# Half pieces of projection work in the latent scan, and an earlier load of attention's operands

## The reference

```python
proj = h @ p['w_in']
q, k, v, z, xbc, dt, gates = jnp.split(proj, SPLIT_IDX, axis=-1)
...
y_f, h_f = ssd_chunked(xs, dt_f, a[0], bm, cm, h0_f)      # scan over chunks of 128 tokens,
y_b, h_b = ssd_chunked(flip(xs), flip(dt_b), ...)         # forward and backward
y = y_f + flip(y_b) + p['d_skip'].astype(jnp.float32)[:, None] * xs
y = rms_norm(y * jax.nn.silu(z), p['ssd_norm'])
g_a, g_b = jnp.split(gates, 2, axis=-1)
merged = jax.nn.sigmoid(g_a) * (attn @ p['w_attn_o']) + jax.nn.sigmoid(g_b) * (y @ p['w_ssd_o'])
```

## Time and profile before

| | us |
|---|---|
| median of 3 runs | 1606.64 |
| the runs | 1606.43, 1606.64, 1609.6 |
| the profiled execution | 1606.35 |
| its span, first to last instruction | 1604.7 |
| PE, DVE, ACT busy in the span | 1545.9, 970.6, 616.4 |
| chunks 1 to 4 on PE, start to start | 52.4, 54.0, 53.9, 46.8 |

### The profile page before, as it was taken

One profiled execution on the slowest core, in us unless ns is written; L12 is line 12 of the kernel. 1 busy time (PEld: TensorE's weight loads), 2 busy tenths in 40 slices (PEclk: granted clock), 3 DMA queues, 4 the chain that ended last, 5 costly groups with the idle time before them and its releaser, 6 DMA issues.

```text
span 1604.7 us, 27065 instructions
## 1 busy us (share of the span) xinstructions
PE 1545.9 (96%) x11130; PEld 1470.5 (92%) x11130; DVE 970.6 (60%) x1359; ACT 616.4 (38%) x1112; POOL 98.7 (6%) x155
## 2 busy tenths in 40 slices
PE   4999999999999999999999999999999999999997
PEld 3899999999999989999655899999999999999997
DVE  5666666668564798898465452448863343442478
ACT  2433333343562366767466343233421121221120
POOL 1001122100101000000000010000000000000000
PEclk9999999999999999999999999999999999999999
DMA  9555455543858668865701345324122222123221
GB/s 318 176 198 189 147 191 171 187 139 103 286 185 287 240 208 281 248 205 168 275 27 45 128 139 186 128 90 163 54 79 79 80 79 80 54 79 106 79 80 66
DMA packets 159910, 241.62 MB, mean 151 GB/s; under 512 B 8080, under 2 KB 126592, under 8 KB 156736
## 3 DMA queue, kind: packets, MB, share of 16 engines
q1 hardware_dynamic: 136624, 171.45, 32.1%
q0 software_dynamic: 12304, 47.72, 8.2%
q10 hardware_dynamic: 10880, 20.97, 5.0%
HBM read 195.06 MB, written 45.06 MB: 150 GB/s over the span
## 4 chain that ended last, share of the span: by engine, by line
PE 84%; DVE 6%; ACT 5%; DMA 2%; issue 1%; SPq 1%; ACTq 0%; DVEq 0%
PE acc L859 67%; PE tp L859 13%; ACT arena L1740 2%; PE tp L1301 1%; DMA arena<-decay_sums_t 1%; DVE wlo L2011 1%; PE tp L987 1%; DMA arena<-in_w_mod 1%; DVE arena L2116 1%; ACT whi L1518 1%; ACT whi L1877 1%; DVE wlo L2467 1%; PE tp L1348 1%; DVE arena L2285 1%; PE tp L898 0%
## 5 line engine op out<-in xcount | busy, mean ns | idle before, releaser
L859 PE MATMUL acc<-hh,whi 128*128 128x322 f32 x1152 | 301.1, 320 | 6.5 <-issue 4.5
L859 PE MATMUL acc<-hl,whi 128*128 128x322 f32 x1152 | 294.8, 315 | 0.0
L859 PE MATMUL acc<-hh,wlo 128*128 128x322 f32 x1152 | 293.5, 313 | 0.0
L859 PEld LDWEIGHTS acc<-hh,whi 128*128 128x128 f32 x1152 | 203.1, 192 | 11.4 <-issue 9.0
L2011 DVE TENSOR_TENSOR wlo<-raw,whi 128x2048 fp32r<-128x2048 f32 x74 | 169.3, 2288 | 61.4 <-ACT whi L1518 61.4
L859 PEld LDWEIGHTS acc<-hl,whi 128*128 128x128 f32 x1152 | 204.6, 192 | 0.0
L859 PEld LDWEIGHTS acc<-hh,wlo 128*128 128x128 f32 x1152 | 204.4, 192 | 0.0
L1518 ACT ACTIVATE whi<-raw 128x2048 fp32r<-128x2048 f32 x74 | 141.1, 1907 | 162.3 <-PE acc L859 161.9
L859 PE MATMUL acc<-whi,hh 128*128 128x256 f32 x640 | 183.1, 286 | 0.0
L859 PE MATMUL acc<-whi,hl 128*128 128x256 f32 x640 | 179.8, 281 | 0.0
L859 PE MATMUL acc<-wlo,hh 128*128 128x256 f32 x640 | 179.7, 281 | 0.0
(11 more groups left out here) (278 smaller groups left out, 2672.4 us busy)
## 6 DMA issues: line engine op xcount, KB each, us to landing
raw<-in_w_in SPq DMA_DIRECT2D x38, 1024.0 KB, 8.6
raw<-in_w_mlp SPq DMA_DIRECT2D x32, 1024.0 KB, 5.3
arena<-in_w_mod SPq DMA_DIRECT2D x24, 1024.0 KB, 8.2
arena<-decay_sums_t ACTq DMA_DIRECT2D x40, 512.0 KB, 6.3
arena<-xs_nat SPq DMA_DIRECT2D x8, 1024.0 KB, 10.6
raw<-in_w_ssd_o SPq DMA_DIRECT2D x8, 1024.0 KB, 6.2
y_nat<-arena POOLq DMA_DIRECT2D x6, 1024.0 KB, 5.6
arena<-y_nat SPq DMA_DIRECT2D x6, 1024.0 KB, 5.9
```

Source lines behind the costliest of these rows:

```text
L859: return pe.matmul(out, l, r, start=first, stop=last)
```

## The change

The table now counts half pieces. `F_LAT` is 4 and `F_LAT_G` = [2, 0, 2, 1, 2, 2, 2, 2]: as before in halves, but for one half more ahead of group 3. That is 17 halves a chunk, 34 pieces in four chunks instead of 32, and `F_END` is 2 instead of 4. A half is the contraction over k = 0 to 3 or 4 to 7 of a piece, 12 matmuls; the waits stand ahead of the first half and the signal behind the second. ACT, DVE, POOL and SP deal with a piece where its second half is (`ended`). In chunks 2 and 4 a call of two halves is the end of one piece and the beginning of the next.

On SP, the loads that belong to the last 8 pieces (two blocks of `w_attn_o`) stand behind attention's loads (`until`). On DVE, `lower_owed` of the last block stands behind the first two row maxima.

```diff
-        F_LAT = [2, 2, 2, 2]
-        F_LAT_G = [1, 0, 1, 0, 1, 1, 1, 1]
-        F_END = N_ZP + N_GP - (F_CTX + sum(F_CTX_G) + F_H0 + 12 * F_BACK + sum(F_LAT) + 4 * sum(F_LAT_G))
+        F_LAT, F_LAT_G = 4, [2, 0, 2, 1, 2, 2, 2, 2]
+        N_PIECES = N_ZP + N_GP
+        F_END = N_PIECES - (F_CTX + sum(F_CTX_G) + F_H0 + 12 * F_BACK + 2 * (F_LAT + sum(F_LAT_G)))
+        def ended(halves, n):
+            k = halves["k"]
+            halves["k"] += n
+            return halves["k"] // 2 - k // 2
...
+            until = N_ZP + N_GP - 8
+            def weights_to_come(n):
+                weights(min(ended(halves, n), until - pieces["k"]))
             for c in range(1, NT):
-                weights(F_LAT[c - 1])
+                weights_to_come(F_LAT)
...
                 for g in range(NG):
-                    weights(F_LAT_G[g])
+                    weights_to_come(F_LAT_G[g])
...
             sp.dma_start(qT[:, 2:HQ], heads[:, 2:HQ]).then_inc(s["av_in"], 16)
-            weights(F_END)
+            weights(N_PIECES - pieces["k"])
...
-            def gate_piece(n):
+            def gate_piece(n, ks=range(KT)):
...
-                if n % 4 == 0:
-                    pe.wait_ge(lo["sem"], due(lo))
-                step(free)
-                pe.wait_ge(free["sem"], value(free, 2))
-                for k in range(KT):
+                if 0 in ks:
+                    if n % 4 == 0:
+                        pe.wait_ge(lo["sem"], due(lo))
+                    step(free)
+                    pe.wait_ge(free["sem"], value(free, 2))
+                for k in ks:
...
-                last.then_inc(ready["sem"], step(ready))
+                if KT - 1 in ks:
+                    last.then_inc(ready["sem"], step(ready))
...
+            def fill_halves(n):
+                for _ in range(n):
+                    ks = (range(0, KT // 2), range(KT // 2, KT))[halves["k"] % 2]
+                    p = pieces["k"]
+                    if p < N_ZP:
+                        z_tile(p, ks)
+                    else:
+                        gate_piece(p - N_ZP, ks)
+                    step(pieces, ended(halves, 1))
...
             for c in range(1, NT):
-                fill(1)
+                fill_halves(2)
...
-                fill(F_LAT[c - 1] - 1)
+                fill_halves(F_LAT - 2)
                 pe.wait_ge(bnin[b]["sem"], due(bnin[b]))
                 for g in range(NG):
-                    fill(F_LAT_G[g])
+                    fill_halves(F_LAT_G[g])
                     scan_group(g, b, c)
...
             weights(F_END)
-            lower_owed()
...
             maxima(0)
             maxima(1)
+            lower_owed()
```

More of the change, by code:

```diff
@@ L579, in z_in @@
                 sp.dma_start(zq[:, q % 2], z_d[c][:, q * 512:(q + 1) * 512]).then_inc(s[f"zq_in{q % 2}"], 16)
+            halves = {"k": 0}
+            until = N_ZP + N_GP - 8
+            def weights_to_come(n):
+                weights(min(ended(halves, n), until - pieces["k"]))
             for c in range(1, NT):
-                weights(F_LAT[c - 1])
+                weights_to_come(F_LAT)
                 if 1 < c < NT - 1:
@@ L824, in _ @@
             stores(4 * F_BACK)
+            halves = {"k": 0}
             for c in range(1, NT):
-                stores(F_LAT[c - 1] + sum(F_LAT_G))
+                stores(ended(halves, F_LAT + sum(F_LAT_G)))
                 if c < NT - 1:
@@ L1096, in _, with z_tile @@
             pieces = count(s["acc_ready"])
-            def z_tile(p):
+            def z_tile(p, ks=range(KT)):
                 slot, t, u = p // NT % 2, p % NT, p % 2
-                if t == 0:
-                    pe.wait_ge(lo["sem"], due(lo))
-                step(free)
-                pe.wait_ge(free["sem"], value(free, 2))
-                for k in range(KT):
+                if 0 in ks:
+                    if t == 0:
+                        pe.wait_ge(lo["sem"], due(lo))
+                    step(free)
+                    pe.wait_ge(free["sem"], value(free, 2))
+                for k in ks:
                     for m, w in ((hh, whi), (hh, wlo), (hl, whi)):
@@ L1791, in _ @@
                     weights(F_BACK)
+            halves = {"k": 0}
             for c in range(1, NT):
                 exps(NG * c)
-                weights(1)
+                weights(ended(halves, 2))
                 if c > 1:
@@ L1797, in _ @@
                 exps(NG * c + 1)
-                weights(1)
+                weights(ended(halves, F_LAT - 2))
                 if c > 1:
                     squares(c - 1, 3, zq[:, 1])
-                weights(F_LAT[c - 1] - 2)
                 for g in range(NG):
-                    weights(F_LAT_G[g])
+                    weights(ended(halves, F_LAT_G[g]))
                     if g + 2 < NG:
@@ L2390, in _ @@
                         gated(c, g // 2 - 2)
-                    weights(F_LAT_G[g] + (F_LAT[c - 1] - (c == 1) if g == 0 else 0))
+                    weights(ended(halves, F_LAT_G[g] + (F_LAT - 2 * (c == 1) if g == 0 else 0)))
                     if g % 2 == 1:
```

## The result

The changed kernel takes 1596.47 us (median of 4 runs, 1595.68 to 1598.1) against 1607.09 for the kernel before on the same chip (4 runs): ratio 0.9932, interval [0.992, 0.9944]. That is 10.6 us less, where 3.7 were forecast (1602.9), and it lies under the range. In a second comparison the same two kernels gave 1596.36 and 1607.39. The profiled execution took 1596.98 us, 9.4 less than that of before.

A forecast was written before the change was run, and what follows sets the result against it. PE was taken as the bound only in part behind group 3, with DVE closing chunk 2. Terms -7.2 -2.2 +2.3 +0.5 +3.7 -1.2 +0.5 = -3.6 us gave 1602.9 us, range 1597.0 to 1608.0.

The forecast's parts named there:

- Two pieces leave the end (-7.2): Between scan and attention: two of four whole gate pieces move into the chunks, -7.2 us if they fit there.
- A half per chunk fits ahead of group 3 at no cost, and the clock stays up behind it: Group 3 of each chunk: a 1.80 us half fits in PE's wait, costs 0, and PE works at full rate behind.
- Chunk 2, the third split (+2.3): End of chunk 2: DVE's added split behind group 7's product delays the next products, +2.3 us, bounds 0 and +2.7.
- rival A: Product waits absent or short because ACT's decay loads land earlier: -10 us, 1596.5; chance 0.27.
- Chunk 3 (+0.5): End of chunk 3: DVE's split behind group 7's product delays the next products, +0.5 us, bounds -1.8 to +1.5.
- chunk 4 (-2.2): Chunk 4: split moves from group 3 to 6, PE keeps full clock; scan ends earlier, -2.2 us, bounds -2.8 and -1.0.
- New waits bring the low clock back: Products of chunks 3 and 4: PE waits about 2.8 and 3.3 us for DVE, then half clock, +3.7, bounds 0 and 7.0.
- leave the 3 us out: Chunk 1: by the skill's micro-idle rule its remaining waits would cost a low-clock stretch, some 3 us, not summed.
- Into attention (-1.2): Behind the last piece: first row maximum runs beside ACT's split, transposes start earlier, -1.2 us, bounds -2.3 and 0.
- The keys' load late (+0.5): Attention's scores: keys land near 763, about when PE needs them, +0.5 us, bounds 0 and 2.5.

The follow-up runs named there:

- the run with 1.83 us of wait: Changed kernel with only attention's loads put back behind the loads of pieces up to 67: 1596.55 us, ratio 0.9933.
- both edits together: Changed kernel with DVE's split behind chunks 2 and 3, SP's last z load earlier, and five halves around products of chunks 3 and 4: 1593.56 us.

## Why the prediction was wrong, step by step

**Two pieces leave the end (-7.2)**: right, 7.21 us for 48 matmuls.

**A half per chunk fits ahead of group 3 at no cost, and the clock stays up behind it**: right in all four chunks of the profile; taking the half out brought waits and half clock back. Chunk 1 gained nothing by it (-0.1), as said: PE then waits again, 1.43 and 1.11 us. In chunk 2 the 3 us that PE was to come early to group 4 stand there as two waits, 1.68 and 1.11 us.

**Chunk 2, the third split (+2.3)**: right in place, over-sized: +1.3. The sum let the last group's product start when it did before, held by ACT. It started 1.1 us earlier than that (648.84, against 649.45 and the 0.45 us by which the chunk began later), since ACT's load of the decays landed sooner. That such loads could land earlier was rival A's reason, and it was set aside with "nothing in the change speeds these loads". With the half taken out they landed later again: the median in the same stretch was 8.4 us, and 6.5 to 7.1 in all twelve profiles of kernels with the halves. So the table does move them, but which transfer makes room was not isolated.

**Chunk 3 (+0.5)** was 0, **chunk 4 (-2.2)** -2.5: within what two profiles differ by.

**"New waits bring the low clock back" (+3.7)**: this is the step that failed, and it carries more than half of the miss of 6.4 us. The waits came where it put them, with the releaser it named, but in the profile at 1.50 and 1.60 us instead of 2.8 and 3.3, and without half clock. In chunk 2, of the 1.3 us that the wait was short, 1.0 is DVE's earlier end and the rest PE's slightly later arrival. In chunk 3 PE arrived 52.27 us after the chunk's start (713.15 less 1.60 less 659.28), where the working had 51.0 (708.6 less 657.56); DVE's last sum ended 0.6 us sooner against it than forecast. The price was wrong too, but less: where the runs forced such a low stretch into chunk 4, it cost 1.3 to 1.6 us and not 2.7. For chunk 3 the 1.0 taken is near the 1.1 that the run with 1.83 us of wait lost against the first profile of the changed kernel (1.9 against the second). So with half clock behind both waits the term would have been some 2.5; with what was there it is 0. It is 0 in the profiled executions, that is: the same waits were once 1.83 us with half clock behind them, as shown above, and the two longest of the changed kernel's nine executions (1598.1 and 1598.68 us) are those with the lowest mean granted clock, 0.996 against 0.997 and 0.998. By our estimate a stretch of 3.4 us at half clock takes 0.001 off that mean (1.7 of 1595 us), but where these two had one is not on record. The mistake in method: a chance event that hangs on a length (does the wait reach what brought half clock?) was put into the sum at full value, on a length that was itself the difference of two forecasts, each off by a microsecond.

The Trainium skill's page "TensorE: Matmul & The Clock Gate", section "A second HAM failure mode: psum-queue depth-cycling", says that frequent micro-idles between groups of matmuls made the clock swing between its levels in a bf16 kernel. Here 1.19, 1.43 and 1.11 us of idle within 11 us, in chunk 1, left it at 1.00 (window 551 to 765 above): for three waits of this size the trace does not bear it out, and the prediction was right to leave the 3 us out.

In the other direction the length of a wait does not decide alone: 1.83, 2.04 and 2.24 us were followed by half clock, 2.33 and 2.59 were not. Nor does the work around it. Behind attention, between 1120 and 1134 us of the span, every kernel here has the same wait of 2.60 us (2.59 to 2.61; the profile names no releaser) ahead of the same matmuls, which the change does not touch. In ten of the fourteen profiles half clock follows it, in four it does not, and the changed kernel has it both ways. Its first profile, PE's timeline and the window behind the wait:

```profile
1124.18 0.38 PE L875 MATMUL acc<-hh,whi 128*128 128x322 f32 x1 [2.60 <-issue]
```

```profile
1124.20:1127.60 3.40, 3.40 (x23) 3.40 (x24) 3.26 (x9) 1.25 (x2) 0.00 (x0) 1.00 0.61 175
```

And the second profile of the same kernel, where 13 matmuls stand in the place of 23:

```profile
1123.67 0.61 PE L875 MATMUL acc<-hh,whi 128*128 128x322 f32 x1 [2.60 <-issue]
```

```profile
1123.70:1127.10 3.40, 3.40 (x13) 3.40 (x14) 3.26 (x9) 1.25 (x2) 0.00 (x0) 0.50 0.60 185
```

So behind a wait of this length half clock comes in some executions and not in others, and what decides it stays open.

**Into attention (-1.2)**: mechanism right, size -2.0 in the profile, 2.2 by the run that undid it. The caution that kept it at half of its bound, PE falling to low clock in the idle time that is left, did not come: the waits were 0.53, 0.97 and 1.64 us, where one of 3.35 us with 3.4 us of half clock behind it stood before (6.8 us of it in the run that undid the move).

**The keys' load late (+0.5)**: 0. It was issued at 754.68, as said, and landed in 6.3 us, not 8.6. Of the three runs that came to the scores 3 to 4 us earlier, two waited for it (1.64 and 1.20 us); the one with the later split did not, because its load was issued at 750.6.

Put together: 1602.9 with -3.7, -1.0, -0.5, -0.3, -0.8 and -0.5 is 1596.1, against 1596.47 measured. Rival A (1596.5, chance 0.27) named the outcome and the reason for the short waits, but its number is in part luck: it took away all of the +2.3 of chunk 2, of which 1.3 stayed, and what made up for it are the terms into attention and of the keys, which it left as they were. The range began at 1597.0, the middle of A's own, and so left half of a case of 27 in 100 outside; its lower end should have been near 1595.

## What to carry to other kernels

Fill the wait ahead of the engine that is the bound with work of just under its length, even half a unit of it: the filler's own time comes off the end, and the clock behind the wait is kept as well; here 7.2 us came off the end for the four halves, and in both profiles of the changed kernel no half clock was left in the scan. Then look what now waits: the two waits that the filling uncovered were worth another 4.4 us by moving one 2.3 us instruction of DVE behind the chunk, and a load of SP with it. In a forecast, do not price a clock loss behind a wait whose length is uncertain by a microsecond as if it were sure: give it a chance, here about one in ten at waits of 0.9 to 1.8 us and ten in fourteen at 2.60, and start the range at the case without it.

## What the runs showed of the hardware

- In the four chunks waits of PE of up to 1.72 us left the granted clock at 1.00 in every profile; of seven different ones between 1.83 and 2.59 us five were followed by half clock (1.83, 2.04, 2.15, 2.24, 2.42) and two were not (2.33, 2.59); all from 2.75 to 4.50 were.
- The same wait at the same place, 2.60 us behind attention, was followed by half clock in ten profiles (kernel before, the changed kernel's second, eight of the experiments) and not in four (the changed kernel's first, no halves, half at group 1, both edits together). At PE's next long wait, some 231 us on, 1.81 us in the changed kernel's first profile brought half clock, while 1.99 and 2.01 us in two of the experiments did not.
- Half clock behind a wait lasted 3.4 or 6.8 us, and the length of the wait does not say which: waits of 3.36 us ahead of the same scores had 3.4 us of it in the run with the table alone and 6.8 in the run with the split back.
- A low stretch of 3.4 us cost 1.3 to 1.6 us in chunk 4 of the scan, about half of PE's busy time in it (3.0 to 3.2 us in the windows behind the products with one and with four products added). Behind the wait of 2.60 us it cost less, 0.9 to 1.1 us: from there to PE's next wait of over 1.5 us passed 231.9 to 232.1 us in the ten profiles that had it and 231.0 in the four that had not.
